# Modulation weights on TensorE's moving side, in pieces of two row chunks by 1024 columns

## The reference, cut to what matters

```python
ada = (jax.nn.silu(c) @ w_ada[layer] + b_ada[layer])[:, None, :]
sh1, sc1, g1, sh2, sc2, g2 = jnp.split(ada, 6, axis=-1)

h = rmsnorm(x, norm_pre_mix[layer]) * (1.0 + sc1) + sh1
proj = h @ w_in[layer] + b_in[layer]
...
x = x + g1 * rmsnorm(mix, norm_post_mix[layer])
h = rmsnorm(x, norm_pre_ffn[layer]) * (1.0 + sc2) + sh2
...
x = x + g2 * rmsnorm(ff, norm_post_ffn[layer])
```

## Time and profile before

| | us |
|---|---|
| median of 3 runs | 2825.66 |
| lowest, highest | 2824.43, 2825.78 |
| profiled execution | 2814.33 |
| its span | 2812.5 |
| PE busy in the span | 2647.3 (94%) |
| DVE busy | 1377.5 (49%) |
| ACT busy | 1039.4 (37%) |
| DMA, mean over the span | 239 GB/s |

### The profile page before, as it was taken

The page is one execution under the profiler, slowest core; times in us unless marked ns, Lnnn a source line. Parts: engine busy times, 40 slices in busy tenths (PEclk is TensorE's granted clock), DMA queues, the critical chain, the costliest instruction groups (busy, mean ns, idle before and its releaser), DMA issues.

```text
span 2812.5 us, 36958 instructions
## 1 busy us (share of the span) xinstructions
PE 2647.3 (94%) x13940; PEld 1856.6 (66%) x13941; DVE 1377.5 (49%) x2613; ACT 1039.4 (37%) x1821; POOL 69.9 (2%) x121
## 2 busy tenths in 40 slices
PE   7999995999999999999998999999998999999999
PEld 7888784334333433343337888788887788788888
DVE  1555763122122112211227869786775666554785
ACT  1343452111111211111125545554654565322653
POOL 0000000000000000000000000000001000010000
PEclk6788995999999999999998999999999999655999
DMA  6554324999999999999984555555555445430553
GB/s 204 167 187 150 120 94 185 392 411 409 404 410 411 408 395 412 408 410 406 410 321 150 191 181 183 165 181 192 182 187 168 147 148 163 101 39 6 165 187 128
DMA packets 329006, 673.42 MB, mean 239 GB/s; under 512 B 8420, under 2 KB 260495, under 8 KB 295968
## 3 DMA queue, kind: packets, MB, share of 16 engines
q1 hardware_dynamic: 325712, 663.40, 64.0%
q0 software_dynamic: 3184, 8.53, 2.2%
HBM read 670.25 MB, written 1.12 MB: 239 GB/s over the span
## 4 chain that ended last, share of the span: by engine, by line
PE 82%; DVE 10%; ACT 4%; issue 2%; DMA 0%; DVEq 0%; POOL 0%; ACTq 0%; POOLq 0%
PE PS L345 22%; PE PS L1193 16%; PE PS L346 11%; PE PS L1210 8%; PE PS L1179 4%; PE PS L687 3%; PE PS L353 3%; DVE WS L308 2%; PE PS L1702 2%; PE PS L1185 2%; PE PS L1723 2%; ACT WS L304 2%; PE PS L354 2%; PE PS L1710 1%; DVE LIN L1307 1%
## 5 line engine op out<-in xcount | busy, mean ns | idle before, releaser
L345 PE MATMUL PS<-HN,WS 128*128 128x512 f32 x1952 | 720.2, 411 | 19.6 <-DVE WS L308 15.4
L308 DVE TENSOR_TENSOR WS<-RAW,WS 128x1024 fp32r<-128x1024 f32 (+1 forms) x452 | 542.5, 1205 | 224.8 <-ACT WS L304 221.2
L346 PE MATMUL PS<-HN,WS 128*128 128x256 f32 x1952 | 558.1, 286 | 0.0
L304 ACT ACTIVATE WS<-RAW 128x1024 fp32r<-128x1024 f32 (+1 forms) x452 | 465.7, 1035 | 158.7 <-PE PS L354 88.7
L345 PEld LDWEIGHTS PS<-HN,WS 128*128 128x128 f32 x1952 | 380.6, 195 | 114.7 <-DVE WS L308 18.9
L1193 PE MATMUL PS<-W,XG 128*64 128x512 f32 x2048 | 449.9, 597 | 0.0
L346 PEld LDWEIGHTS PS<-HN,WS 128*128 128x128 f32 x1952 | 382.8, 196 | 0.5
L1303 DVE TENSOR_SCALAR GLU<-PS 128x512 f32<-128x512 f32 x32 | 22.1, 692 | 728.5 <-PE PS L1193 728.5
L1193 PEld LDWEIGHTS PS<-W,XG 128*64 128x64 f32 x2048 | 144.9, 138 | 303.5 <-issue 303.5
L1210 PE MATMUL PS<-W,AT 128*64 128x512 f32 x1024 | 226.8, 595 | 22.0 <-ACT AT L1111 22.0
L345 PE MATMUL PS<-MI,WS 128*128 128x512 f32 x704 | 245.4, 394 | 0.0
(11 more groups left out here) (335 smaller groups left out, 2956.9 us busy)
## 6 DMA issues: line engine op xcount, KB each, us to landing
W<-in_moe_w SPq DMA_DIRECT2D x192, 2048.0 KB, 10.6
RAW<-in_ffn_w_in SPq DMA_DIRECT2D x88, 1024.0 KB, 5.1
RAW<-in_attn_w_qkv SPq DMA_DIRECT2D x36, 1024.0 KB, 5.1
RAW<-in_ffn_w_out SPq DMA_DIRECT2D x32, 1024.0 KB, 5.0
RAW<-in_w_ada SPq DMA_DIRECT2D x24, 1024.0 KB, 7.6
RAW<-in_w_in SPq DMA_DIRECT2D x22, 1024.0 KB, 5.2
RAW<-in_ffn_w_out SPq DMA_DIRECT2D x16, 768.0 KB, 4.3
RAW<-in_conv_w_in SPq DMA_DIRECT2D x12, 1024.0 KB, 5.1
```

What stands on the lines that cost most here:

```text
L304: act_f(split_tile(0, n), raw_tile(n), ACT.Copy).then_inc(hi_done, 1)
L308: vec.tensor_tensor(split_tile(1, n), raw_tile(n), split_tile(0, n).bitcast(f32), ALU.subtract).then_inc(lo_done, 1)
L345: nc.tensor.matmul(both, hi[:, k, :], x2[:, :, kx, :], start=start, stop=False)
L346: ins = nc.tensor.matmul(half, lo[:, k, :], x2[:, 0, kx, :], start=False, stop=stop)
```

## The change

A piece is now two chunks of 128 rows by 1024 columns, again 1 MB, in runs of 4 KB. Piece j belongs to part r = j // 4 and holds the row chunks 2q and 2q + 1 with q = j % 4; the order in the stream and the places of the pieces on PE are as before. The weights are the moving operand. The stationary one is a chunk of `silu(c)`, widened to 32 columns of which the first holds the numbers and 31 are zero (`CWIDE`, filled by POOL). The 1024 columns of a chunk go as four matmuls of 256 columns to four quarters of the array, 32 columns each (`tile_position`), which write to 32 partitions each. So a piece has 8 matmuls in place of 16. The result of a part is one row in four stretches, on partitions 0, 32, 64 and 96. ACT copies it to SBUF (`row_of_ada`), PE turns it with two transposes (`turn_ada`), and DVE adds the bias (`take_ada`), part by part: parts 0 and 1 in the prologue, parts 2 to 5 at s = 8, 16, 24 and 32.

The table rows leave the prologue on PE and ACT. They now stand at s = 0, 1 and 2, one each, and share a bank with the mean; POOL's part is unchanged.

```diff
+    CWIDE = Region(spare0 + 6 * KB)("CWIDE", [DC, 32])
...
             if kind == "ada":
-                sp.dma_start(RAW[G % 4][:, :, :], w_ada[:, :, 2 * P * i:2 * P * (i + 1)]).then_inc(raw_loaded[G % 4], 16)
+                sp.dma_start(ada_tile(i), w_ada[:, i % 4 * 2:i % 4 * 2 + 2, D * (i // 4):D * (i // 4 + 1)]).then_inc(raw_loaded[G % 4], 16)
...
+        nc.gpsimd.memset(CWIDE[:, :, :], 0.0).then_inc(sem("filled"), 1)
...
-        act_f(CSIL[:, :], PRM[:, COL["c"]:COL["c"] + DC], ACT.Silu).then_inc(sem("silu_c"), 1)
+        act_f(CWIDE[:, :, 0], PRM[:, COL["c"]:COL["c"] + DC], ACT.Silu).then_inc(sem("silu_c"), 1)
...
         def act(act):
-            for g in range(N_GROUPS):
+            def table_rows(g):
                 act.wait_ge(sem("rows_mm"), g + 1)
-                act_f(RT[0:HEADS, g, :], bank[g][0:HEADS, 0:384], ACT.Copy).then_inc(sem("rows_ready"), 1)
+                act_f(RT[0:HEADS, g, :], bank[6][0:HEADS, 0:384], ACT.Copy).then_inc(sem("rows_ready"), 1)
+
+            def row_of_ada(r):
+                act.wait_ge(sem("ada_mm"), 4 * r + 4)
+                act_f(AROW[:, r % 2, :], ada_bank(r)[:, 0:S], ACT.Copy).then_inc(sem("ada_row"), 1)
...
             first_splits(act, win, hi_tile)
+            row_of_ada(0)
+            row_of_ada(1)
...
             def behind(s):
+                if s < N_GROUPS:
+                    table_rows(s)
+                if s in (7, 15, 23, 31):
+                    row_of_ada(2 + s // 8)
...
             def ada(j):
+
+                r, q = j // 4, j % 4
                 wait_raw(pe, "ada", j)
-                w = RAW[raw_slot("ada", j)]
-                for c in range(2):
-                    for k in range(DC):
-                        last = nc.tensor.matmul(bank[5][:, 2 * j + c:2 * j + c + 1], w[:, k, c * P:(c + 1) * P],
-                                                CSIL[:, k:k + 1], start=k == 0, stop=k == DC - 1)
+                if q == 0 and r >= 3:
+                    pe.wait_ge(sem("ada_taken"), r)
+                w = ada_tile(j)
+                for k in range(2):
+                    for g in range(4):
+                        last = nc.tensor.matmul(ada_bank(r)[32 * g:32 * g + 32, 0:S], CWIDE[:, 2 * q + k, :],
+                                                w[:, k, S * g:S * (g + 1)], start=q == 0 and k == 0,
+                                                stop=q == 3 and k == 1, tile_position=(0, 32 * g))
                 last.then_inc(sem("ada_mm"), 1)
+
+            def turn_ada(r):
+                pe.wait_ge(sem("ada_row"), r + 1)
+                pe.wait_ge(sem("small_loaded"), 16)
+                for h in range(2):
+                    last = nc.tensor.transpose(ada_bank(r)[:, S + h * P:S + (h + 1) * P], AROW[:, r % 2, h * P:(h + 1) * P], IDENT)
+                last.then_inc(sem("ada_turned"), 1)
 
             def gates(c):
                 if c == 0:
                     pe.wait_ge(sem("bd_loaded"), 32)
-                    pe.wait_ge(sem("root_done"), 1)
+                    pe.wait_ge(sem("rows_ready"), N_GROUPS)
...
             def behind(s):
-                if s % 2 == 1 and ADA_FIRST + s // 2 < ADA_PAIRS:
+                if s < N_GROUPS:
+                    table_rows(s)
+                if s % 2 == 1 and ADA_FIRST + s // 2 < ADA_PIECES:
                     ada(ADA_FIRST + s // 2)
+                if s in (8, 16, 24, 32):
+                    turn_ada(1 + s // 8)
...
             for j in range(ADA_FIRST):
                 ada(j)
-            pe.wait_ge(sem("ada_ready"), 1)
+            turn_ada(0)
+            turn_ada(1)
...
-                if s == 33:
-                    dve.wait_ge(sem("ada_mm"), ADA_PAIRS)
-                    take_ada(2, 6, ((1, 2, "norm_post_mix", 0.0), (2, 4, "norm_pre_ffn", 1.0), (3, 5, "norm_post_ffn", 0.0)))
+                if s in (8, 16, 24, 32):
+                    r = 1 + s // 8
+                    take_ada(r)
+                    if r != 3:
+                        gain, plus = {2: ("norm_post_mix", 0.0), 4: ("norm_pre_ffn", 1.0), 5: ("norm_post_ffn", 0.0)}[r]
+                        modulate(max(1, r - 2), r, gain, plus).then_inc(sem("ada_ready"), 1)
```

More of the change, by code:

```diff
@@ L250, in block_program @@
     stops = sorted({by_name[x].n0 for x in fresh if by_name[x].n0} | {n})
-    ADA_PAIRS = 24
+    ADA_PIECES = 24
     ADA_FIRST = 8
@@ L262, in stream_order @@
                 order += [("ada", j) for j in range(ADA_FIRST)]
-            elif n >= 4 and ADA_FIRST + n // 2 - 2 < ADA_PAIRS:
+            elif n >= 4 and ADA_FIRST + n // 2 - 2 < ADA_PIECES:
                 order.append(("ada", ADA_FIRST + n // 2 - 2))
@@ L267, in block_program, with ada_tile @@
     place_of = {item: G for G, item in enumerate(stream)}
+    def ada_tile(j):
+        return RAW[place_of["ada", j] % 4][:, :, :].rearrange("p k n -> p (k n)").rearrange("p (k n) -> p k n", k=2)
     def load_stream(sp, G0, G1):
@@ L518, in mixer @@
         WT = Region(ub0)("WT", [4, S])
+        AROW = Region(spare0 + 4 * KB)("AROW", [2, S])
         DIST = Region(spare0)("DIST", [S])
@@ L537, in of, with ada_bank @@
             return PROJ[:, WIN_PART[t], :]
+        def ada_bank(r):
+            return bank[7] if r == 1 else bank[5]
         def pool(pool):
@@ L670, in pe @@
         def pe(pe):
[L671 to L675, removed]
+            pe.wait_ge(sem("filled"), 4)
             pe.wait_ge(sem("squared"), 1)
@@ L680, in pe, with table_rows @@
             pe.wait_ge(sem("silu_c"), 1)
+            def table_rows(g):
+                pe.wait_ge(sem("rb_loaded"), 32)
+                if g:
+                    pe.wait_ge(sem("rows_ready"), g)
+                nc.tensor.matmul(bank[6][0:HEADS, 0:384], RB[0:BUCKETS + 1, g * HEADS:(g + 1) * HEADS],
+                                 OH[0:BUCKETS + 1, g, :], start=True, stop=True).then_inc(sem("rows_mm"), 1)
             def ada(j):
+                r, q = j // 4, j % 4
                 wait_raw(pe, "ada", j)
-                w = RAW[raw_slot("ada", j)]
-                for c in range(2):
-                    for k in range(DC):
-                        last = nc.tensor.matmul(bank[5][:, 2 * j + c:2 * j + c + 1], w[:, k, c * P:(c + 1) * P],
-                                                CSIL[:, k:k + 1], start=k == 0, stop=k == DC - 1)
-                last.then_inc(sem("ada_mm"), 1)
+                if q == 0 and r >= 3:
[6 more added lines that the diff above has]
+                                                stop=q == 3 and k == 1, tile_position=(0, 32 * g))
+                last.then_inc(sem("ada_mm"), 1)
+            def turn_ada(r):
[4 more added lines that the diff above has]
+                last.then_inc(sem("ada_turned"), 1)
             def gates(c):
@@ L813, in dve, with take_ada, modulate @@
             o.link(TS(SINK[:, 1, :], SINK[:, 0, :], -1.0, None, ALU.mult))
[L815 to L825, removed]
+            def take_ada(r):
+                dve.wait_ge(sem("ada_turned"), r + 1)
+                turned = ada_bank(r)[:, S:2 * S].rearrange("p (h g x) -> p g h x", h=2, g=4)[:, :, :, 0]
+                ins = TTN(ADA[:, r * DC:(r + 1) * DC].rearrange("p (g h) -> p g h", g=4), turned,
+                          PRM[:, COL["b_ada"] + r * DC:COL["b_ada"] + (r + 1) * DC].rearrange("p (g h) -> p g h", g=4), ALU.add)
+                ins.then_inc(sem("ada_taken"), 1)
+                dve.wait_ge(sem("ada_taken"), r + 1)
+            def modulate(r, part, gain, plus):
+                return STT(ADV[:, r, :], ADA[:, part * DC:(part + 1) * DC], plus,
+                           PRM[:, COL[gain]:COL[gain] + DC], ALU.add, ALU.mult)
+            take_ada(0)
+            take_ada(1)
+            modulate(0, 1, "norm_pre_mix", 1.0).then_inc(sem("ada_ready"), 1)
             dve.wait_ge(sem("scaled"), DC)
```

6 lines of the change are left out of this document (3 added, 3 removed).

## The result

| | before | after |
|---|---|---|
| median, us | 2825.05 (4 runs, 2818.68 to 2825.78) | 2755.13 (4 runs, 2752.79 to 2760.67) |
| ratio, 95% interval | | 0.976 (0.9739 to 0.9782) |
| profiled execution, its span | 2814.33, 2812.5 | 2752.79, 2751.0 |

The forecast was 2759, 67 us less. In what follows the marks of the mixer are compared (the start of a tile's first product, or of `gates(0)`, in a trace), since the kernels differ only there. Tiles are counted as in `win`, from 0 to 43. What lies behind the mixer varied from one profiled execution to the next, with the same work, from 2377 to 2388 us; a difference of a few us between two spans says nothing by itself.

The account below looks back on a forecast made before the run. PE was taken as the bound: one-column matmuls fill it in the prologue and halve the clock behind them in `win`. Savings 25.1 + 11.4 + 5.0 + 24.7 + 0.8 = 67 from 2825.7 gave 2759 us, range 2744 to 2782.

Parts of the forecast that it names:

- The piece: Each new piece on PE: four quarters run together, 1.1 us at full clock and 1.9 at half.
- Prologue: Before the first product of `win`: earlier squares, then transfers as the limit; start at 47.5 for 77.70, 30.2 us earlier.
- From tile 0 to `gates(0)`: First `win` product to PE's arrival at `gates(0)`: tiles 0 to 3, table products and two pieces, 47.5 to 66.7.
- The wait for `BDX`: Before `gates(0)`: PE waits 10.4 us for POOL's late store and load, `BDX` landing at 77.1; bounds 3 to 13.
- Gates: s = 3 to 10: gate products, seven tiles and three pieces take 32 us for 43.4, saving 11.4.
- Tiles 11 to 17: s = 11 to 17: ACT's and DVE's work ends last, two pieces lie hidden under it; 5.0 us saved of 45.8.
- the turns: PE's transposes of a part's row: 0.5 us in the gates, 1.5 for three with their waits in s = 18 to 31.
- The peak: DVE's first attention maximum, within s = 11 to 17: 1.4 us saved before it, 3.6 after it.
- Tiles 18 to 31: s = 18 to 31, seven pairs of tiles with a piece each: 70.3 us for 95.0, saving 24.7.
- The pair: Two tiles and a piece in s = 18 to 31: 8.3 us from the `wor` stage plus 1.1, for 13.6 before.
- the gelu: s = 29 to 31: DVE's and ACT's long operations, covered before, come into the open and add 3 us.
- The drain at a change of tiling mode: Each piece changes mode twice: 0.3 us dearer, 4 us for 14 open pieces, making 2763 in place of 2759.

Follow-up runs that it names:

- e8: Changed kernel with the four matmuls of a row chunk given to two array quarters in turn: median 2760.33 us (other numbers reach the routing), a piece 1.92 us.
- e9: Changed kernel with all matmuls of a piece in one array quarter: median 2809.75 us (other numbers reach the routing), a piece 3.64 us.
- e3: Changed kernel with the three table rows back at the start of the prologue on PE and ACT: ratio 0.9751 to the kernel before.
- the control: The changed kernel run again, unedited, beside later follow-up runs on one chip: median 2758.38 us, ratio 0.9769 to the kernel before.
- e1: Changed kernel with POOL issuing the loads of BDA, BDX and DIST ahead of the table rows' store: median 2742.03 us, ratio 0.9734.
- e2: Changed kernel with take_ada at the head of DVE's side work for each s, in place of the end: ratio 0.9759 to the kernel before.
- e6: Changed kernel with take_ada first and, for s = 14 to 16, DVE's attention ahead of the recurrence's long operations: median 2745.7 us, ratio 0.9729.
- e4: Changed kernel with pieces 8 to 23 computed as 16 one-column matmuls each, as before: median 2893.67 us, but with 35 expert blocks for 32.

## Why the prediction was right, step by step

- **The piece** (1.1 us at full clock, 1.9 at half): 1.07 and 1.94. That four quarters run together was inferred from L1193's halves; e8 and e9 show it.
- **Prologue** (-30.2): -30.5. The squares start at 6.50 (6.6), the transfer of piece 2 at 21.98 (22), the first product at 47.21 (47.5). e3, which undoes the early start, has the first product 7.1 later, where the prediction counts 7.5.
- **From tile 0 to `gates(0)`** (19.2): 19.3 here, but 21.9 in the control and 22.0 in e1, at a clock of 0.77 for 0.91. That the mark fell on the forecast to 0.2 us is in part luck.
- **The wait for `BDX`** (10.4): 12.26. The chain is as the prediction put it, from the third row at 63.8 through the store (4.8 for 5.3) to `BDX`, mis-sized by 2.2: 9.2 us to landing for 7.0. By the Trainium skill's page "DMA: Bandwidth & Descriptors" (its table of fixed and variable time) it would have been 3.2, an estimate. This transfer, issued 0.6 us behind `BDA` and with 289 GB/s moved by the core's DMA in this window in all, took three times that, and 9.6 in e1.
- **Gates** (32): 32.6, about 1 of it PE's wait for `take_ada(2)` before piece 12, which the forecast has at nothing.
- **Tiles 11 to 17** (5.0 saved): nothing saved, the one step that failed. That ACT's and DVE's work sets the pace there was seen. Missed was the wait that the change adds on PE, `ada_taken` before piece 16: the transposed row of part 3 is read by DVE at the end of its work for s = 16, behind scans and attention. I counted the turns at 0.5 each and never asked what stood before `take_ada` on DVE. It cost 2 to 3.3 us (e2). The peak itself did not fail the forecast: it came 2.4 us earlier in relation to tile 11 (27.7 us after its start, 30.1 before), for 1.4 forecast. What failed lies behind it, up to tile 18: 18.4 us, 15.7 before, 12.1 forecast. Tile 16 is not shorter there (6.87 and 6.88), and tile 17, with piece 16's wait and PE at half clock behind it, is 2.7 longer (10.5 for 7.8). Of these 6.3 us the wait is shown; the rest, PE waiting for DVE's work in its old order and the clock behind each wait, is argued from the traces, and e6 shows that the order of that work was worth 4.6.
- **Tiles 18 to 31** (24.7 saved): 28.8. The pair was taken too long, 9.4 for 8.95, which is 3 us in seven pairs; why a pair of the `wor` stage, from which it came, is longer is not shown. And of the 3 us for the gelu 1.6 showed in the stretch (tile 31 took 6.7 for the 5.1 of other tiles with a piece). Behind it the last row of the first table is 2.0 longer, 1.0 in the control; that this is the gelu's remainder is not shown.
- **The clock** carries as much as the matmuls do. The 31.5 us by which tiles 18 to 31 are shorter than with old pieces (e4) fall, by e9, into 16.3 through the clock and 15.2 through shorter pieces. The kernel before took 2.7 less there than e4, so for the change itself the split is not exact.
- **The drain at a change of tiling mode** (the Trainium skill, "TensorEngine Tiling (Array Packing)", Key Properties; weighed as 0.3 us a piece on top of 1.1): a piece starts at 165.33, 0.21 behind the product before it, where such products are otherwise 0.12 apart, and the next product starts at 166.33. So it holds PE for 1.00 + 0.09 = 1.09 us, of which its four rounds fill 4 x 0.214 = 0.86. The 0.23 left for both changes are near the rule's 0.3 and are the 0.2 that the forecast has for start and end: the rule's price was in the 1.1 already, and 2759, not 2763, was the sum to use.
- Sum: 67 forecast; 60.7 in the mixer, 61.5 between the profiled executions, 69.9 between the medians, and 64.5 between the medians of the control's comparison. The errors of the steps (2 lost up to the start of `gates(0)`, 1 in the gates, 5 at tiles 11 to 17, 3 behind tile 32, 4 gained at tiles 18 to 31) make 6 to 7 less than forecast, and that is what the mixer shows. The median of 2755 for 2759 is closer than the steps deserve, and that is luck: the forecast took the median's distance from the profiled execution to stay as it was, 11.3, and after the change it was 2.3.

## What to carry to other kernels

For a product of one row with a large float32 matrix, try the matrix as the moving operand, its columns spread over the four column quarters of the array: here a piece of 1 MB took 1.07 us in place of 3.63. Ask of small matmuls not only what they last, but what clock the products behind them get. And when work is moved out of a prologue, follow every queue that hung on it: here a store ahead of a load on POOL cost 12 us, and issuing the load first took that wait away. The same goes for each new wait: ask what stands in the other engine's queue ahead of the instruction that ends it.

## What the runs showed of the hardware that I had not expected

TensorE's clock follows what kind of work fills it too, and not only whether it is busy: with 3.63 us of one-column matmuls in each pair of tiles it stood at 0.81 while PE was busy for 97.1 of 97.7 us (e4), with 3.64 us of 256-column matmuls in a quarter of the array at 1.00, busy for 80.9 of 81.5 (e9). In the prologue, where a piece of 1.9 us comes every 3 us, it stood at 0.50:

```profile
23.50:44.00 20.50, 11.18 (x96) 3.57 (x96) 0.81 (x2) 0.38 (x1) 0.00 (x0) 0.50 1.00 370
```

With the same matmuls in one quarter of the array, and PE so busy for 24.2 of 26 us, it stood at 0.90 there (e9). Which of the two decides is not shown.

The same opening of 102 matmuls ran at 0.77 in one execution and 0.85 in another. In single traces this is worth 3 us, as much as some of the effects sought.
